# How the matmul engine releases used expert weight buffers in a two-block transformer kernel

## The reference

```python
def hier_moe(h, w_rg, b_rg, w_re, b_re, w_gate, w_up, w_down):
    ...
    y = jnp.zeros_like(h)
    for e in range(N_EXPERTS):               # 16 experts, 4 groups of 4, 2 chosen in one group
        hid = jax.nn.silu(h @ w_gate[e]) * (h @ w_up[e])     # 1024 x 256 each
        y = y + gates[..., e:e + 1] * (hid @ w_down[e])      # 256 x 1024
    return y
```

## Time and profile before

| | |
|---|---|
| median of three runs | 2679.83 us |
| profiled execution, its own time | 2685.11 us |
| span of the profiled execution | 2683.3 us |
| mean granted TensorE clock | 0.982 of full speed |
| PE busy over the span | 2574.9 us (96%) |
| DVE, ACT, GpSimd busy | 1281.9, 1086.4, 884.3 us |
| first and last matmul of the experts' units | 408.9 us, 698.3 us |

### The profile page before, as it was taken

One profiled execution on the slowest core, in us unless ns is written; L12 is line 12 of the kernel. 1 busy time (PEld: TensorE's weight loads), 2 busy tenths in 40 slices (PEclk: granted clock), 3 DMA queues, 4 the chain that ended last, 5 costly groups with the idle time before them and its releaser, 6 DMA issues.

```text
span 2683.3 us, 30652 instructions
## 1 busy us (share of the span) xinstructions
PE 2574.9 (96%) x12190; PEld 2069.3 (77%) x12190; DVE 1281.9 (48%) x1823; ACT 1086.4 (40%) x1696; POOL 884.3 (33%) x390
## 2 busy tenths in 40 slices
PE   8988999999899999999999999999999999999997
PEld 6768787777776788878788888766888878788886
DVE  2984357777558656544431010576457353510112
ACT  3344225666336547333332122347374233322231
POOL 4470100000131344433244344321444432344344
PEclk9998989999999999999999999999999999999999
DMA  6232338899521233323233333221333331233232
GB/s 209 87 91 59 104 131 307 315 358 342 194 86 40 63 94 102 95 95 102 72 92 115 100 94 102 72 63 35 99 95 98 115 110 56 80 101 116 89 95 78
DMA packets 220077, 318.80 MB, mean 119 GB/s; under 512 B 17184, under 2 KB 176032, under 8 KB 219808
## 3 DMA queue, kind: packets, MB, share of 16 engines
q1 hardware_dynamic: 201184, 284.24, 32.8%
q10 hardware_dynamic: 16592, 24.72, 2.7%
q0 software_dynamic: 2160, 7.89, 0.8%
HBM read 301.06 MB, written 15.75 MB: 118 GB/s over the span
## 4 chain that ended last, share of the span: by engine, by line
PE 87%; DVE 10%; ACT 1%; issue 1%; DMA 1%; DVEq 0%; ACTq 0%
PE ps L670 80%; PE ps L829 4%; PE ps L682 3%; DVE stats L2119 1%; DVE ix L2232 1%; DVE top L2230 1%; DVE rows L2129 1%; DVE pair_l L2406 1%; DMA rows<-in_x 0%; ACT pair_h L1716 0%; DVE rows L2141 0%; DVE qf L2497 0%; DVE nmax L2076 0%; DMA gain_f<-in_ln_b_f 0%; DVE vbuf L2495 0%
## 5 line engine op out<-in xcount | busy, mean ns | idle before, releaser
L611 POOL TENSOR_TENSOR w_lo<-w_raw,w_hi 128x1024 fp32r<-128x1024 f32 x331 | 812.7, 2465 | 1405.8 <-ACT w_hi L1478 1405.8
L670 PE MATMUL ps<-x_hi,w_hi 128*128 128x512 f32 x1624 | 647.7, 399 | 5.3 <-DVE x_lo L2036 4.4
L670 PE MATMUL ps<-x_hi,w_lo 128*128 128x512 f32 x1624 | 634.2, 391 | 0.0
L670 PE MATMUL ps<-x_lo,w_hi 128*128 128x512 f32 x1624 | 633.7, 390 | 0.0
L1478 ACT ACTIVATE w_hi<-w_raw 128x1024 fp32r<-128x1024 f32 x331 | 341.4, 1053 | 503.3 <-PE ps L670 480.7
L670 PEld LDWEIGHTS ps<-x_hi,w_hi 128*128 128x128 f32 x1624 | 305.7, 188 | 89.6 <-issue 20.9
L670 PEld LDWEIGHTS ps<-x_lo,w_hi 128*128 128x128 f32 x1624 | 305.8, 188 | 64.8
L670 PEld LDWEIGHTS ps<-x_hi,w_lo 128*128 128x128 f32 x1624 | 306.2, 189 | 63.3 <-issue 2.9
L2642 DVE TENSOR_TENSOR fhd<-fsg,ps 128x512 f32<-128x512 f32 x44 | 30.2, 688 | 383.0 <-PE ps L670 382.9
L2406 DVE TENSOR_TENSOR pair_l<-pair_raw,pair_h 128x2048 fp32r<-128x2048 f32 x84 | 189.8, 2288 | 46.6 <-ACT pair_h L1716 46.5
L1716 ACT ACTIVATE pair_h<-pair_raw 128x2048 fp32r<-128x2048 f32 x84 | 157.8, 1910 | 3.2 <-ACT yb L1731 2.8
(11 more groups left out here) (403 smaller groups left out, 4326.1 us busy)
## 6 DMA issues: line engine op xcount, KB each, us to landing
w_raw<-in_w_in SPq DMA_DIRECT2D x102, 512.0 KB, 3.7
w_raw<-in_ffn_wi SPq DMA_DIRECT2D x88, 512.0 KB, 3.5
pair_raw<-in_w_gate SPq DMA_DIRECT2D x56, 512.0 KB, 5.6
pair_raw<-in_w_up SPq DMA_DIRECT2D x56, 512.0 KB, 6.9
pair_raw<-in_w_down SPq DMA_DIRECT2D x56, 512.0 KB, 6.4
w_raw<-in_ffn_wo SPq DMA_DIRECT2D x44, 512.0 KB, 3.6
w_raw<-in_w_out SPq DMA_DIRECT2D x24, 512.0 KB, 3.6
kv_raw<-in_ckv_w SPq DMA_DIRECT2D x20, 512.0 KB, 3.8
```

Source lines behind the costliest of these rows:

```text
L611: pool.tensor_tensor(w_lo[:, slot, :], w_raw[:, slot, :], w_hi[:, slot, :].bitcast(F32), ALU.subtract).then_inc(lo_done, 1)
L670: ins = pe.matmul(o, a, b, start=first, stop=last)
```

## The change

`free_pair` no longer issues a drain; it sets a flag, and the next matmul or transpose that PE issues through `mm` or `flip` carries the `pair_used` signal when it has no other. A new `free_now` does the drain where no such matmul follows at once: ahead of the `kv` slab in steps 8, 10, 12 and 14, and behind the last step. Nothing changes on the other engines.

```diff
@@ mm and flip
-            used_later = [False]
+            used_later, pair_later = [False], [False]
...
                 if inc is not None:
-                    assert not used_later[0]
+                    assert not used_later[0] and not pair_later[0]
                     ins.then_inc(s[inc], 1)
                 elif used_later[0]:
                     ins.then_inc(slab_used, 1)
                     used_later[0] = False
+                elif pair_later[0]:
+                    ins.then_inc(pair_used, 1)
+                    pair_later[0] = False
@@
             def free_pair():
-                pe.drain().then_inc(pair_used, 1)
+
+                pair_later[0] = True
+
+            def free_now():
+                if pair_later[0]:
+                    pe.drain().then_inc(pair_used, 1)
+                    pair_later[0] = False
@@ the loop over steps
                 if step in (8, 10, 12, 14):
+                    free_now()
                     if step == 8:
                         pe.wait_ge(s["first_gates_copied"], 1)
...
+            free_now()
             kv(26)
             kv(27)
             barrier()
```

## The result

The changed kernel takes 2655.89 us in the median of 4 runs (2651.82 to 2660.26). The kernel before, measured beside it, takes 2679.80 us (2678.80 to 2684.73). The ratio is 0.9911, 95% interval 0.9899 to 0.9924: 23.9 us or 0.9% faster, clear of the 0.2% that a measurement can tell. The forecast was 2658.4 us, in a range of 2653.5 to 2666.5. The profiled execution took 2660.26 us (span 2658.5); against the profiled one before that is 24.9 us less, where the sum had said 21.4.

A forecast was written before the change was run, and what follows sets the result against it. PE was taken to bound the experts' stage, losing time at drains. 35 x 0.50 + 6 x 0.43 = 20.1, plus 1.4 at block ends, gave 21.4 us with rounding; 2679.83 - 21.4 = 2658.4 us, range 2653.5 to 2666.5.

The forecast's parts named there:

- the sum: Experts' stage: 51 drains less 10 leave 41, 35 x 0.50 + 6 x 0.43, plus 4 x 0.34: 21.4 us saved.
- What bounds the stage: Experts' stage: PE sets the pace, busy 56.85 of 60 us; 52 waits for "issue", 33.7 us, are the drains.
- The price of one drain: At PE's drains: 0.42 us plus 0.08 for the matmul behind, 0.50 us; 0.43 ahead of a block's eight transposes.
- Satisfied waits cost nothing and the drain costs all of it.: At PE's seams: starts 0.23 us apart with satisfied waits and no drain, 0.65 with a drain.
- The count and the signal's new place: In PE's loop: 28 + 23 = 51 drains go; the signal riding on a matmul costs 0.00 us.
- The plain unit: Between two units' transposes: 9.48 falls to 8.48 us; the feed ring takes 7.5, PE arrives last with 1 us to spare.
- The four block ends and the last unit: Steps 5, 17, 21, 25: PE waits until about 6.57 us, two drains give 0.34; in unit 27 they give 0.
- The loads: Weight loads in the stage: four units in 35.6 us need 382 GB/s; 418 was seen, so no cost.
- the DMA rival: Loads in the stage: share 0.95 at 350 GB/s limits them to 368 GB/s; 7 us lost, 2665.4 us; chance 0.09.
- The feed: Plain units: if the ACT and DVE ring were 9.0 us, not 7.5, 14 us less saved, 2672 us; chance 0.08.
- The gap: At PE's seams, rival: 0.65 us comes from the sequencer meeting waits, so the time stays 2679.8 us; chance 0.05.
- Slower: At half 1's release: ACT standing there closes a ring, 0.3 us per unit lost, 8.4 in all, 2688 us; chance 0.02.

The follow-up runs named there:

- the test in half 0: Changed kernel plus one bare drain per unit in the middle of half 0, with two long-satisfied semaphore waits behind it: 2665.64 us in one run, stage 277.9 us.
- The kernel with the late signal: Changed kernel, but half 1's release rides on the eleventh of the twelve down matmuls, not the first: 2662.43 us in one run, stage 269.4 us.
- Splitting first: Changed kernel, but at a block's end ACT splits the down pair before it copies `yb`: 2648.42 us in one run, stage 265.7 us.
- The kernel with two products: Kernel with the three repairs and SP's new load order, but gate and up leave out the tokens' low-part product: 2624.94 us in one run.
- extra drain: Changed kernel plus one bare drain per unit in the middle of half 0, no waits behind it: 2665.20 us in one run, stage 274.4 us.
- loads early in the changed kernel: Changed kernel, but SP loads the next block ahead of the down pair and each key and value slab one unit later: stage 266.1 us.

## Why the prediction was right, point by point

**What bounds the stage.** Right. The 52 waits for "issue" were the drains: 5 are left, and bare drains bring the gaps back.

**The price of one drain.** 0.50 us was said; 0.53 was measured (the transposes of steps 3 and 4 start at 437.93 and 446.36 us in the changed kernel, 8.43 apart, against 9.48 in the earlier trace rows). The 0.03 are the matmuls behind the first two, which stay a little slower for some rows. Ahead of the transposes of a block I had said 0.43; it was 0.50 (466.74 to 467.78 is 1.04 us, against 1.54).

**"Satisfied waits cost nothing and the drain costs all of it."** This step failed in its reasoning, though not in the sum. The waits are free between half 0 and the transposes (0.23 us), and behind a drain they are not: 0.47 us without waits, 0.58 with two, 0.61 at the seams, 0.65 with the drain's own signal. So the 0.42 of excess is 0.24 drain, 0.11 exposed waits and 0.04 signal; 0.03 between the test in half 0 and the seams stays open. That PE's sequencer reaches the waits ahead of time where there is no drain is my reading of this; the runs show only the cost. The sum held because all of it went with the drain.

**The count and the signal's new place.** 51, and 0.00: both right. The kernel with the late signal shows that there is slack: 2.3 us later cost PE about 1 us in the whole stage.

**The plain unit.** I said 8.48 us with PE last to arrive; it is 8.43, with no wait of PE in it.

**The four block ends and the last unit.** Right in place and size: 6.57 us were forecast from the last down matmul to the next product, 6.55 came; the waits stand in steps 5, 17, 21 and 25. Unit 27's distance is 5.33 us in both kernels (666.62 to 671.95). Splitting first makes the four waits go, which shows their cause.

**The sum.** 21.4 us forecast, 22.8 in the stage: 35 drains at the measured 0.53 and 6 at 0.50 are 21.6, the block ends add 4 x 0.36 = 1.4, together 23.0; 0.1 of the difference is the block's load in step 10. The term of the sum that was mis-sized is the price of a drain, by 0.03 us, and by 0.07 for the six ahead of a block's transposes. The rest of the 23.9 in the medians, and of the 24.9 in the profiled pair, lies outside the stage, where nothing was changed; no run settles more than that it varies.

**The loads.** 382 GB/s were said to be needed, and 381 ran, at a share of 1.01. Nothing was lost there, so the DMA rival falls, and so does its inference from the share: 0.95 at 350 GB/s did not mean 5% of room. The kernel with two products moved 419 GB/s for 40 us. By the 358 GB/s that the Trainium skill gives in "DMA: Bandwidth & Descriptors", section Specifications, neither could be; its page "HBM Reference", section Specifications (TRN2), has it that a core that streams alone gets about 425, and with that the trace agrees (419). The part of the DMA rival that was right is the burst behind the slabs: 0.12 us in the changed kernel, 1.7 once PE is faster still.

**The other rivals.** The feed never paced a plain unit. The gap was the drain. Slower would have needed ACT to stand at the release, and ACT stood there only when the signal was made 2.3 us later; even then it cost PE about 1 us in all.

## What to carry to other kernels

Let the next instruction carry a release instead of draining for it, and price the drain from the distances between starts around one: here 0.53 us each, of which a drain alone makes 0.34; most of the rest is its signal and waits that cost nothing without it. Before counting such savings, follow each one to the next thing that is due: at four block ends two drains together gave 0.36 us and not 1.06, at the end of the stage nothing. And when a total disagrees with the theory, or agrees with it, compare the single gaps first: the split in front of `yb` gave its 3.2 us and lost 2.8 in two other places, the late signal seemed to cost 2.9 us where 1.6 were the clock, and the two waits behind a drain met their forecast by 1.2 us of the same.

## What the runs showed of the hardware

In six kernels PE waits 2.00 us ahead of the last down product. The granted clock fell behind that wait in three (late signal, split first, drain with two waits) and stayed at 1.00 in the other three (changed kernel, extra drain, loads early in the changed kernel); where it fell, the product took 1.2 to 1.6 us longer. No run shows what decides it. A DMA share of 1.01 went with 381 GB/s and 1.03 with 418 and 419, so the share tells that the engines have work, not how much more they could move.
